# Smaller first loads and two projection units computed side by side at the start of a two-layer encoder kernel

## The reference

```python
h = rms_norm(x, norm_mix[layer])            # x * rsqrt(mean(x*x) + EPS) * gain
qa, ka, va, ra, ga, qb, kb, vb = split_cols(h @ w_in, AB_SPLITS)
# layer 0: gated linear attention on (qa, ka, va, ra, ga), stick-breaking attention on (qb, kb, vb)
# then output projection, residual, norm, conv feed-forward; layer 1: sliding-window attention, the same feed-forward
```

## Time and profile before

| | |
|---|---|
| time, median of 3 runs | 1179.33 us (1178.47 to 1180.39) |
| span of the profiled execution (first to last instruction) | 1176.8 us |
| TensorE busy | 1150.4 us, 98% |
| VectorE busy | 654.7 us, 56% |
| ScalarE busy | 490.5 us, 42% |
| first product of a unit starts | 9.33 us |
| vb 1 starts | 28.02 us |

### The profile page before, as it was taken

One profiled execution on the slowest core, in us unless ns is written; L12 is line 12 of the kernel. 1 busy time (PEld: TensorE's weight loads), 2 busy tenths in 40 slices (PEclk: granted clock), 3 DMA queues, 4 the chain that ended last, 5 costly groups with the idle time before them and its releaser, 6 DMA issues.

```text
span 1176.8 us, 15063 instructions
## 1 busy us (share of the span) xinstructions
PE 1150.4 (98%) x5402; PEld 936.2 (80%) x5402; DVE 654.7 (56%) x840; ACT 490.5 (42%) x706; POOL 8.6 (1%) x25
## 2 busy tenths in 40 slices
PE   8999999999999999999999999999999999999995
PEld 7776767778888888888888878778888888888884
DVE  5334333565777767773333564465777777763333
ACT  5557443744434444443332355444444434432220
POOL 1000000000000000000000000000000000000000
PEclk9999999999999999999999999999999999999998
DMA  5211211122232222223334212032222232223321
GB/s 222 72 55 54 72 54 37 54 90 90 90 107 89 95 101 89 102 62 101 96 98 143 77 54 88 19 106 90 91 95 101 89 107 89 85 81 99 98 85 71
DMA packets 31750, 102.91 MB, mean 87 GB/s; under 512 B 3537, under 2 KB 3682, under 8 KB 31714
## 3 DMA queue, kind: packets, MB, share of 16 engines
q1 hardware_dynamic: 30978, 100.17, 26.3%
q10 hardware_dynamic: 736, 2.24, 0.6%
HBM read 99.84 MB, written 2.10 MB: 87 GB/s over the span
## 4 chain that ended last, share of the span: by engine, by line
PE 63%; issue 31%; ACT 3%; DVE 2%; DMA 1%; POOLq 0%; POOL 0%; DVEq 0%; ACTq 0%; SPq 0%
PE ps L1139 18%; PE ps L1141 18%; PE ps L1140 18%; PE ps L1303 2%; PE ps L1290 2%; PE ps L1311 1%; PE ps L1407 1%; PE ps L1431 1%; PE ps L1362 1%; DMA x<-xT 1%; ACT pr L805 1%; PE ps L1417 0%; ACT w_hi L593 0%; DVE x L1127 0%; PE ps L1192 0%
## 5 line engine op out<-in xcount | busy, mean ns | idle before, releaser
L593 ACT ACTIVATE w_hi<-w_raw 128x1024 fp32r<-128x1024 f32 (+1 forms) x203 | 198.2, 976 | 518.7 <-PE ps L1141 518.7
L829 DVE TENSOR_TENSOR w_lo<-w_raw,w_hi 128x1024 fp32r<-128x1024 f32 (+1 forms) x205 | 229.8, 1121 | 244.7 <-ACT w_hi L593 238.8
L1139 PE MATMUL ps<-h_hi,w_hi 128*128 128x512 f32 x896 | 355.5, 397 | 6.2 <-DVE h_lo L844 2.6
L1141 PE MATMUL ps<-h_hi,w_lo 128*128 128x512 f32 x896 | 349.5, 390 | 0.0
L1140 PE MATMUL ps<-h_lo,w_hi 128*128 128x512 f32 x896 | 349.4, 390 | 0.0
L1139 PEld LDWEIGHTS ps<-h_hi,w_hi 128*128 128x128 f32 x896 | 168.6, 188 | 46.0 <-issue 10.3
L1141 PEld LDWEIGHTS ps<-h_hi,w_lo 128*128 128x128 f32 x896 | 168.4, 188 | 35.7
L1140 PEld LDWEIGHTS ps<-h_lo,w_hi 128*128 128x128 f32 x896 | 168.7, 188 | 34.8 <-issue 1.2
L1139 PE MATMUL ps<-y_hi,w_hi 128*128 128x512 f32 x352 | 136.9, 389 | 0.0
L1140 PE MATMUL ps<-y_lo,w_hi 128*128 128x512 f32 x352 | 136.9, 389 | 0.0
L1141 PE MATMUL ps<-y_hi,w_lo 128*128 128x512 f32 x352 | 136.9, 389 | 0.0
(11 more groups left out here) (177 smaller groups left out, 1082.4 us busy)
## 6 DMA issues: line engine op xcount, KB each, us to landing
w_raw<-w_up SPq DMA_DIRECT2D x88, 512.0 KB, 3.3
w_raw<-w_mix SPq DMA_DIRECT2D x53, 512.0 KB, 3.3
w_raw<-w_down SPq DMA_DIRECT2D x32, 384.0 KB, 3.1
w_raw<-w_down SPq DMA_DIRECT2D x32, 320.0 KB, 2.9
out<-x SPq DMA_DIRECT2D x8, 256.0 KB, 2.2
x<-xT SPq DMA_DIRECT2D x2, 512.0 KB, 8.0
x<-xT ACTq DMA_DIRECT2D x2, 512.0 KB, 8.3
bias_sb<-bias ACTq DMA_DIRECT2D x1, 512.0 KB, 4.9
```

What stands on the lines that cost most here:

```text
L593: s.activation(w_hi[r % SPL][:, 0:cols], w_raw[r][:, 0:cols], ACT.Copy).then_inc(w_hi_ready, 1)
L829: v.tensor_tensor(w_lo[r % SPL][:, 0:cols], w_raw[r][:, 0:cols], w_hi[r % SPL][:, 0:cols].bitcast(F32), ALU.subtract).then_inc(w_lo_ready, 1)
L1139: mm(dst, w[0], m[0], start=first, stop=False, skip_group_check=shared)
L1141: return mm(dst, w[1], m[0], start=False, stop=last, skip_group_check=shared)
```

## The change

Three things are altered, all of them at the start of the program.

1. Transfers. x comes in eight pieces of one block (256 KB) with a semaphore each, units 0 and 1 in halves of four blocks (256 KB). SyncE issues the first half of unit 0, x 1, x 2, the second half of unit 0, x 4, the second half of unit 1, x 5, x 6, x 7, units 2 and 3. ScalarE issues the gains alone (44 of the 404 columns of `par`), x 0, the first half of unit 1, x 3; the other columns of `par` are issued by ScalarE behind its last `h_hi`, and waited for ahead of the first GELU.
2. Splits. Units 0 and 1 are split in halves, and the halves of unit 1 follow one block behind those of unit 0.
3. Order. TensorE computes qb 0 and kb 0 together: block c of qb 0, then block c of kb 0. Both `sq` steps stand behind both units, and with them behind the splits of units 2 and 3.

```diff
-    seq = q[:4] + k[:4] + ev("sq", 0) + q[4:] + ev("sq", 1) + k[4:]
+    seq = sum((q[c:c + 1] + k[c:c + 1] for c in range(KC)), []) + ev("sq", 0) + ev("sq", 1)
...
+        W_HALVES = (slice(0, UC // 2), slice(UC // 2, UC))
+
+        def load_x(engine, c):
+
+            engine.dma_start(x[:, c, :], xT[:, c * T:(c + 1) * T]).then_inc(x_loaded[c], 16)
+
+        def load_half(engine, u, half):
+
+            engine.dma_start(w_raw[u][:, W_HALVES[half]], w_mix0[u][:, W_HALVES[half]]).then_inc(
+                w_loaded[u] if half else half_loaded[u], 16)
...
-            for u in range(RAW):
+            load_half(sp, 0, 0)
+            load_x(sp, 1)
+            load_x(sp, 2)
+            load_half(sp, 0, 1)
+            load_x(sp, 4)
+            load_half(sp, 1, 1)
+            for c in (5, 6, 7):
+                load_x(sp, c)
+            for u in (2, 3):
                 sp.dma_start(w_raw[u][:, :], w_mix0[u]).then_inc(w_loaded[u], 16)
-                if u < 2:
-                    i = 3 * u
-                    sp.dma_start(x[:, 2 * i:2 * i + 2, :], x_pair(i)).then_inc(x_loaded[i], 16)
...
-            act.dma_start(par[:, :], small).then_inc(par_loaded, 16)
-            for i in (1, 2):
-                act.dma_start(x[:, 2 * i:2 * i + 2, :], x_pair(i)).then_inc(x_loaded[i], 16)
-
+            act.dma_start(par[:, 0:S_CONV], small[:, 0:S_CONV]).then_inc(gains_loaded, 16)
+            load_x(act, 0)
+            load_half(act, 1, 0)
+            load_x(act, 3)
+
+            def half_hi(u, half):
+
+                act.wait_ge(w_loaded[u] if half else half_loaded[u], 16)
+                s.activation(w_hi[u][:, W_HALVES[half]], w_raw[u][:, W_HALVES[half]],
+                             ACT.Copy).then_inc(w_hi_ready if half else half_hi_ready, 1)
...
+            act.dma_start(par[:, S_CONV:S_END], small[:, S_CONV:S_END]).then_inc(par_loaded, 16)
...
-                if span[0] == 0:
+                if in_halves and span[0] == 0:
+                    pe.wait_ge(half_lo_ready, u + 1)
+                if span[0] == (KC // 2 if in_halves else 0):
                     pe.wait_ge(w_lo_ready, u + 1)
```

More of the change, by code:

```diff
@@ L345, in trunk @@
         unit_done = sem("unit_done")
-        x_loaded = [sem(f"x_loaded{i}") for i in range(4)]
+        x_loaded = [sem(f"x_loaded{c}") for c in range(KC)]
+        gains_loaded = sem("gains_loaded")
+        half_loaded = [sem(f"half_loaded{u}") for u in range(2)]
+        half_hi_ready = sem("half_hi_ready")
+        half_lo_ready = sem("half_lo_ready")
         par_loaded = sem("par_loaded")
@@ L480, in trunk @@
         NADD = KC + 1
-        def x_pair(i):
-            return xT[:, 2 * i * T:(2 * i + 2) * T].rearrange("p (c t) -> p c t", t=T)
+        W_HALVES = (slice(0, UC // 2), slice(UC // 2, UC))
[4 more added lines that the diff above has]
+                w_loaded[u] if half else half_loaded[u], 16)
         def o1_psum(b):
@@ L609, in rinv_copy @@
                 s.activation(rinv[:, :], ps[:, B_RINV, :], ACT.Copy).then_inc(rinv_ready, 1)
-            act.dma_start(par[:, :], small).then_inc(par_loaded, 16)
-            for i in (1, 2):
-                act.dma_start(x[:, 2 * i:2 * i + 2, :], x_pair(i)).then_inc(x_loaded[i], 16)
+            act.dma_start(par[:, 0:S_CONV], small[:, 0:S_CONV]).then_inc(gains_loaded, 16)
[6 more added lines that the diff above has]
+                             ACT.Copy).then_inc(w_hi_ready if half else half_hi_ready, 1)
             for c in range(KC):
-                if c % 4 == 0:
-                    act.wait_ge(w_loaded[c // 4], 16)
-                    s.activation(w_hi[c // 4][:, :], w_raw[c // 4][:, :], ACT.Copy).then_inc(w_hi_ready, 1)
+                if c % 4 < 2:
+                    half_hi(c % 4, c // 4)
                 if c == 0:
-                    act.wait_ge(par_loaded, 16)
-                if c % 2 == 0:
-                    act.wait_ge(x_loaded[c // 2], 16)
+                    act.wait_ge(gains_loaded, 16)
+                act.wait_ge(x_loaded[c], 16)
                 s.activation(h_hi[:, c, :], x[:, c, :], ACT.Copy, scale=gain_at(0, c)).then_inc(hi_ready, 1)
+            act.dma_start(par[:, S_CONV:S_END], small[:, S_CONV:S_END]).then_inc(par_loaded, 16)
             def b_evac(dst, n_cols, src, next_a=0):
@@ L702, in ffn @@
                 act.wait_ge(warmed, layer)
+                act.wait_ge(par_loaded, 16)
                 s.activation(gelu_warm[:, :], par[:, 0:1], ACT.Gelu_apprx_tanh).then_inc(warmed, 1)
@@ L871, in _, with half_lo @@
             v.memset(ssq[:, :], 0.0).then_inc(ssq_added, 1)
+            def half_lo(u, half):
+                dve.wait_ge(w_hi_ready if half else half_hi_ready, u + 1)
+                cols = W_HALVES[half]
+                v.tensor_tensor(w_lo[u][:, cols], w_raw[u][:, cols], w_hi[u][:, cols].bitcast(F32),
+                                ALU.subtract).then_inc(w_lo_ready if half else half_lo_ready, 1)
             for c in range(KC):
-                if c % 4 == 0:
-                    lo_static(c // 4)
+                if c % 4 < 2:
+                    half_lo(c % 4, c // 4)
                 h_lo_part(0, c)
@@ L1145, in w_blocks, with a_unit @@
                 return tuple(t[r % SPL][:, c * n:(c + 1) * n] for t in (w_hi, w_lo))
-            def a_unit(u, r, bank, h_blocks=None, span=(0, KC)):
-                if span[0] == 0:
+            def a_unit(u, r, bank, h_blocks=None, span=(0, KC), in_halves=False):
+                if in_halves and span[0] == 0:
+                    pe.wait_ge(half_lo_ready, u + 1)
+                if span[0] == (KC // 2 if in_halves else 0):
                     pe.wait_ge(w_lo_ready, u + 1)
@@ L1277, in _ @@
                             pe.wait_ge(b_taken, b_done - TT + 1 if after_group else b_done)
-                        a_unit(i, i, a_bank0(a), 0 if i < 2 else None, span)
+                        a_unit(i, i, a_bank0(a), 0 if i < 2 else None, span, i < 2)
                 elif name == "ssq":
```

## The result

| | before | changed |
|---|---|---|
| median | 1179.33 us | 1183.30 us |
| all runs | 1177.48 to 1181.38 (7) | 1181.71 to 1183.97 (7) |
| ratio | | 1.0029 (1.0018 to 1.0041) |
| span of the profiled execution | 1176.8 us | 1179.9 us |

The changed kernel is **slower by 0.3%**, 4.0 us in the medians (the ratio, taken over all the runs, is 3.4 us). The forecast was 1179.3 with 1181.7 as the upper end: it missed by 4.0, and the measured time lies outside its range. The sign that it gave the most weight (no change) was wrong too.

A forecast was written before the change was run, and what follows sets the result against it. TensorE, busy 98% of the span, was taken as the bound. A 3.8 us head start was used up by new holes of 1.9 and 1.7 us: vb 1 at 28.0 against 28.02, so 1179.3 us, range 1178.0 to 1181.7.

The forecast's parts named there:

- the earlier start: First product of qb 0 on TensorE at 7.0 instead of 9.33; both units together end 3.8 us sooner.
- the hole ahead of vb 0: TensorE waits 1.9 us, 18.1 to 19.95, for vb 0's weight splits, which need qb 0's buffer.
- the second hole ahead of the sums: After vb 0, TensorE waits 1.7 us, 25.4 to 27.15, for VectorE's additions of squares queued behind splits.
- the distance of vb 1 from qb 0's last product: vb 1 starts 10.6 us after qb 0's last product, through splits, additions and column sums.
- rival (a): Head start survives: squares or sums not late, vb 1 at 24.4, 3.6 us won, 1175.7; chance 0.05.
- x block 0 at 4.9: At the start, ScalarE's first x piece, behind 22 KB of gains, lands at 4.9 by equal shares of bandwidth.
- each microsecond goes through: Each microsecond that the start is earlier or later passes to the end, through qb 0's last product.
- a first product at 8 or later: Sign in the next profile that the forecast landings are wrong; first product was expected near 7.0.
- the point of no change at 17.4: If qb 0's last product ends at 17.4, vb 1 starts at 28.0, against 28.02 before: time unchanged.
- the base: Start of vb 1 in the profile of the kernel before, 28.02, on which the sum was made.
- Rival (b): The clock falls once in a new hole of 1.9 or 1.7 us, costing 1.7 us: 1180.9; chance 0.17.
- Rival (d): 256 KB pieces on SyncE's queue pay one by one, 2.2 us each; qb ends at 23.3: 1185.2; chance 0.02.

The follow-up runs named there:

- the two readings: The changed kernel measured twice, the second time unchanged: 1183.30 us, ratio 1.0029, then 1182.21 us, ratio 1.0023.
- x 0 first: Changed kernel with x block 0 issued ahead of the gains on ScalarE's queue: 1182.27 us, ratio 1.0022.
- filled holes: Changed kernel with products of ones on TensorE, 8 ahead of vb 0 and 7 ahead of the column sums: 1181.94 us, ratio 1.0016.
- more warming: Changed kernel with 22 warming products on TensorE instead of 14: 1182.43 us, ratio 1.0031.
- before with the new tail: Kernel before, own transfers and whole splits; only blocks 4 to 7 of qb and kb side by side, both square steps behind: 1184.93 us, ratio 1.0046.

## Why the prediction was wrong, step by step

**What held.** Which terms there are: the earlier start, the hole ahead of vb 0 (1.9 forecast; 1.79 by the trace), the second hole ahead of the sums (1.7; 1.67 in the profiles at the full clock), the distance of vb 1 from qb 0's last product (10.6; 10.75), and that vb 1 hangs on that product alone. The sentence on rival (a) held as well: with the queue order changed back the head start survives.

**The step that failed first** is in the part on loads and the start: x block 0 at 4.9. It landed at 6.5, the first product started at 8.21 instead of 7.0, and qb 0 ended at 18.95 instead of 17.4. By the prediction's own rule ("each microsecond goes through") these 1.55 us, with 0.15 more in the distance, are the delay of vb 1, 1.7. It had itself named a first product at 8 or later as the sign that the landings are wrong. I had shared the bandwidth by bytes, and given the gains the weight of their 22 KB. They cost x block 0 about 1.1 of the 1.6 us; the rest is that the first pieces never landed together, wherever the gains stood. Between 4.0 and 6.0 us the changed kernel moved 264 and 313 GB/s, where before moved 419 and 410:

```profile
4.00:5.00 1.00, 1.00 (x8) 1.00 (x8) 0.00 (x0) 0.48 (x2) 0.76 (x5) 1.00 0.99 264
5.00:6.00 1.00, 1.00 (x12) 1.00 (x11) 0.69 (x1) 0.15 (x1) 0.17 (x2) 1.00 0.93 313
```

All ten profiles with the new transfers are that low (202 to 272 and 207 to 356 GB/s), with the gains in any of the four places, so their place isn't the cause of that; the smaller pieces and the shorter rows of `par` came together, and no run tells them apart. With x 0 at 4.9 the forecast of no change would, by the same rule, have been near for this profile; no run of the changed order started that early. The range I gave the start, 0.5 early to 1 late, was too narrow for a landing that no row showed: the point of no change at 17.4 was hit so exactly that any error became the sign. And 1178.3 to 1180.3 leaves no room for both errors that it names: a start 1 late and a run 1 high give 1181.3.

**The second failed step** is the base. I took 28.02 from the one profile, in which the clock had fallen behind the 2.6 us hole, and let the change win those 1.4 us back. In a part of the runs of before the clock doesn't fall there (the 19 of 85 above). Compared at the full clock throughout, the changed kernel is some 3 us late: vb 1 at 29.70, which its fall didn't move (10.75 behind qb 0's end, as without a fall), against 28.02 - 1.4 = 26.6 for before. That is also what the terms give: two waits of 1.94 and 1.83 us from where the next product could have started (19.47 to 21.41 in the changed kernel, 27.46 to 29.29 in the run with x 0 first), 0.3 lost inside the pair, less 1.1 of earlier start. And the runs give it: the one run of the changed kernel with a granted clock above 0.993 (0.996) has a span of 1178.8 us, and the five at 0.995 of the same order with filled holes have 1178.7 to 1179.4; the 19 of before have 1176.0 on average, some 3 us less. The medians of the two readings differ by 4.0 and 3.1 us.

**Rival (b)** was right in kind, wrong in its sum. The clock did fall right behind the first hole, in the profiles at 21.8 and 22.2, and cost almost nothing there: the slower vb 0 ended when the additions did (28.76 and 28.67), so the fall filled the second hole. What costs in full is a fall behind the second hole (at 30.4 and 31.4, in the run with more warming and in before with the new tail). That such falls are a part of the changed kernel's loss is argued from the filled holes (ratio 1.0016 against 1.0029 and 1.0023), not shown: no profile of the changed kernel itself has one. How often the clock falls at either place I can't tell from one or two profiles per kernel; that stays open.

The Trainium skill (DMA: Bandwidth & Descriptors, Bandwidth) asks for transfers of 1 MiB or more. Pieces of 256 KB did move less between 4 and 6 us, the 264 and 313 GB/s above, but 385 to 412 GB/s from 6 us on, where before had 410 to 422. The prediction's estimate from the Trainium skill, 2.6 us a piece, one behind the other, was not seen here: ScalarE starts on the last of SyncE's nine pieces at 12.97, not near 25. Rival (d) is out. The Trainium skill (TensorE: Matmul & The Clock Gate, Part 1) says that the moment at which the clock rises differs between runs of the same kernel; here the moment of a fall did, 8.9 and 10.0 in the two profiles of before, 21.8 and 22.2 in those of the changed kernel.

## What to carry to other kernels

When two units share buffers with what comes next, their end times are resources: computing them side by side starts both earlier and ends the first one later, and everything that waits for its buffer waits with it; ask what cover stands between the end of the first and the consumer of its buffer. Work that needs nothing (here the squares) must not stand in a queue behind a wait, but all of it ahead is as bad: put in front only what fits in the idle time. And where a forecast comes out at zero as the difference of terms of 4 us, its range is that of the worst-known term, not that of the difference.

## What the runs showed of the hardware

- The granted clock can fall to 1.2 GHz without any hole: all 14 profiles have 32 products of 64x64 in 3.4 to 3.5 us, and in 9 of them it falls within 0.5 us of their end. Each fall behind vb 1 cost 1.5 us of the span.
- A fall followed a hole of 1.8 us in three profiles (at 21.8, 22.2 and 23.0) and not in three others (x 0 first, more warming, before with the new tail). It costs nothing when a later wait absorbs it: vb 1 starts 10.75 us behind qb 0's end with it and 10.76 without.
- With a piece of 128 rows of 176 bytes (22 KB) ahead of it on its queue x block 0 (256 KB) landed about 1 us later (6.4 to 6.7 us against 5.5 or less), 0.4 of it the issue. Queued behind a 256 KB piece, the 22 KB took 5.6 and 4.5 us themselves.
